# Value projection of the second attention: weights stationary, then transposed, with VectorE writing the rows

## The reference, cut to what matters

```python
def shared_kv(h, w_kv, f_bias, k_gain):
    k, v, fl = jnp.split(h @ w_kv, [B_W, 2 * B_W], axis=-1)
    k = rms_norm(k.reshape(B, T, B_HEADS, HEAD_DIM), k_gain)
    v = v.reshape(B, T, B_HEADS, HEAD_DIM)
    log_f = jax.nn.log_sigmoid(fl + f_bias)
    c = jnp.cumsum(log_f, axis=1).transpose(0, 2, 1)
    return k, v, c

def fox_attention(h, w_q, q_gain, w_out, k, v, c):
    q = rms_norm((h @ w_q).reshape(B, T, B_HEADS, HEAD_DIM), q_gain)
    ...   # scores + decay from c, causal mask, softmax, p @ v, then @ w_out
```

## Time and profile before

| | |
|---|---|
| time, 3 runs | 2240.07 us median (2239.18 to 2240.89) |
| span of the profiled execution | 2240.1 us |
| PE busy | 2018.0 us (90%) |
| DVE busy | 1583.8 us (71%) |
| ACT busy | 1114.1 us (50%) |
| mean granted TensorE clock | 0.984 |

### The profile page before, as it was taken

How to read it: one execution, slowest core, us unless ns; L and a number is a source line. 1 busy time by engine, 2 the same in 40 slices (tenths; PEclk the granted TensorE clock), 3 DMA queues, 4 the chain that set the end, 5 groups by cost and what they waited for, 6 DMA issues and landing times.

```text
span 2240.1 us, 28570 instructions
## 1 busy us (share of the span) xinstructions
PE 2018.0 (90%) x9930; PEld 1294.1 (58%) x9930; DVE 1583.8 (71%) x3680; ACT 1114.1 (50%) x2715; POOL 629.8 (28%) x621
## 2 busy tenths in 40 slices
PE   8899999999999989888779989988999998788876
PEld 7789999789999975433234434433444443233322
DVE  7857778768788888666676586567567666776655
ACT  5456436466534465454445475444356544444543
POOL 0000011100011044344333343344234344444442
PEclk9899999999999999999999999999999999999999
DMA  6226698726598579999999999999999999999997
GB/s 236 77 92 204 221 343 284 256 84 212 195 357 303 188 282 419 421 421 421 421 421 421 421 416 417 414 421 418 398 418 404 421 421 421 421 421 405 422 420 292
DMA packets 130773, 764.58 MB, mean 341 GB/s; under 512 B 14416, under 2 KB 16208, under 8 KB 59088
## 3 DMA queue, kind: packets, MB, share of 16 engines
q0 software_dynamic: 87552, 587.24, 64.3%
q1 hardware_dynamic: 42368, 174.15, 21.4%
q10 hardware_dynamic: 720, 1.51, 0.2%
HBM read 761.80 MB, written 1.05 MB: 341 GB/s over the span
## 4 chain that ended last, share of the span: by engine, by line
PE 50%; DMA 30%; DVE 11%; ACT 5%; issue 3%; POOL 1%; DVEq 0%; POOLq 0%; ACTq 0%
DMA arena<-experts,arena 27%; PE bank L1092 14%; PE bank L599 9%; PE bank L601 8%; PE bank L600 8%; PE bank L1130 6%; DVE arena L2686 3%; DMA wring<-w_stream 1%; DVE wlo L1993 1%; DMA arena<-ada_w 1%; ACT arena L1711 1%; PE bank L783 1%; ACT arena L1495 1%; POOL arena L570 1%; ACT arena L1710 1%
## 5 line engine op out<-in xcount | busy, mean ns | idle before, releaser
L1092 PE MATMUL bank<-arena 128*128 128x512 f32 x2048 | 975.8, 615 | 161.7 <-ACT arena L1711 159.9
L2686 DVE CUSTOM_DVE_ANT_0 arena<-arena 128x1024 f32<-128x1024 f32 x512 | 626.3, 1225 | 449.7 <-DMA arena<-experts,arena 448.9
L570 POOL DMA_INDIRECT arena<-experts,arena x512 | 565.7, 1105 | 841.3 <-PE bank L1092 782.1
L1092 PEld LDWEIGHTS bank<-arena 128*128 128x128 f32 x2048 | 372.7, 193 | 716.3 <-issue 360.8
L1706 ACT ACTIVATE arena<-arena 128x1 f32<-128x1 f32 x512 | 103.4, 202 | 583.3 <-DVE arena L2686 581.4
L1382 ACT CAST whi<-wring 128x1024 fp32r<-128x1024 f32 x229 | 239.1, 1050 | 226.3 <-PE bank L601 220.9
L1993 DVE TENSOR_TENSOR wlo<-wring,whi 128x1024 fp32r<-128x1024 f32 x229 | 278.9, 1223 | 68.7 <-ACT whi L1382 67.9
L1711 ACT ACTIVATE arena<-tab,arena 128x128 f32<-128x128 f32 x512 | 205.5, 401 | 16.7
L550 POOL DMA_DIRECT2D arena<-ada_w x64 | 34.4, 537 | 575.0 <-DVE adaM L2040 561.8
L599 PE MATMUL bank<-hTh,whi 128*128 128x256 f32 (+1 forms) x584 | 169.9, 291 | 1.9 <-DVE wlo L1993 1.3
L601 PE MATMUL bank<-hTh,wlo 128*128 128x256 f32 (+1 forms) x584 | 165.2, 283 | 0.0
(11 more groups left out here) (407 smaller groups left out, 2903.2 us busy)
## 6 DMA issues: line engine op xcount, KB each, us to landing
wring<-w_stream SPq DMA_DIRECT2D x233, 512.0 KB, 4.3
wring<-w_stream SPq DMA_DIRECT2D x46, 1024.0 KB, 9.1
arena<-ada_w POOLq DMA_DIRECT2D x64, 512.0 KB, 5.5
alibi<-ada_w POOLq DMA_DIRECT2D x32, 512.0 KB, 5.6
arena<-experts,arena POOLq DMA_INDIRECT x512
xT<-xT_in SPq DMA_DIRECT2D x2, 544.0 KB, 4.3
alibi<-alibi_in ACTq DMA_DIRECT2D x1, 1024.0 KB, 6.0
tab<-tab_in SPq DMA_DIRECT2D x1, 847.0 KB, 10.5
```

Source lines behind the costliest of these rows:

```text
L570: pool.indirect_dma_start(g_ring[:, r], None, experts[n // (2 * PEER_HEADS)], bass.IndirectOffsetOnAxis(idx[:, s // SLOTS % 2, s % SLOTS:s ...
L1092: last = mm(banks[2 * t + b][:, :], diag[:, r], g_ring[:, r, D + b * TILE_N:D + (b + 1) * TILE_N], start=s % SLOTS == 0, stop=s % SLOTS == ...
L2686: v.tensor_tensor_reduce(g_ring[:, r, 0:D], g_ring[:, r, 0:D], hrow[:, t], 1.0, 0.0, ALU.mult, ALU.add, act8[:, r:r + 1]).then_inc(dot_don ...
```

## The change

The weights become the stationary operand. `value_chunk(n)` makes 128 value columns for all 272 tokens with 24 matmuls, so there are eight chunks instead of 12 groups. ScalarE copies each chunk, unscaled, to a new double-buffered tile `vTB` (`value_copied`). TensorE turns it by three transposes into a bank (`value_turn`), and VectorE multiplies by `kv_ri` and writes `vB` (`value_scaled`, two instructions). The six scaled ScalarE copies go. The order around this is rewritten on the three engines. The release of the ring's chunks for tiles 27 and 28 goes from two halves to each chunk. In the changed program the lines after the new code have other numbers: 600 to 602 are the three matmuls, 986 `head_spread`, 1037 the transposes, 2017 `split_lo`, 2064 `ada_part`, 2383 `head_scale`, 2401 to 2405 `decay_rows`, 2432 and 2433 `value_scaled`.

```diff
-CHUNK_FREE.update({g: (2, 2, 4, 4) for g in (G_BV, G_BV + 1)})
...
+        vTB = m(2, T)
...
-        BV_BANKS = ((0, 1, 2), (4, 7, 6))
+        VALUE_BANK = (0, 1, 2, 3, 6, 7, 6, 7)
+        TURN_BANK = (4, 4, 4, 4, 4, 5, 4, 6)
...
                     if layer and n == 0:
-                        pe.wait_ge(v_ready, 7)
+                        pe.wait_ge(v_ready, 10)
...
             beside_values = attention(1)
-            for n in range(12):
-                x, half, r = n // 6, n // 3 % 2, n % 3
...
-                rows(G_BV + x, c0, TILE_N // 2, banks[BV_BANKS[x][r]][0:nq, c0:c0 + TILE_N // 2],
-                     parts(kvh, kvl, q0, q0 + nq), ((0, 0, 2), (1, 0, 1))[half][r])
-                if n == 0:
-                    head_sums(14)
-                if n < 2:
-                    head_spread(6 + n)
-                elif n < 6:
-                    head_spread(2 * n + 4)
-                    head_spread(2 * n + 5)
-                elif n == 6:
...
-                    next(beside_values)
-                elif n == 8 or n == 10:
-                    next(beside_values)
+            def value_chunk(n):
...
+                chunk(G_BV + n // CPT, n % CPT, banks[VALUE_BANK[n]][:, 0:T], kv_all)
+            def value_turn(n):
...
+                else:
+                    pe.wait_ge(v_ready, 3 + (CPT + 1 if n == CPT + 2 else n))
+                pe.wait_ge(z_copied, 17 + n)
+                for r, (q0, nq) in enumerate(ROWS):
+                    last = nc.tensor.transpose(banks[TURN_BANK[n]][0:nq, r * P:(r + 1) * P], vTB[:, n % 2, q0:q0 + nq], ident)
+                last.then_inc(kv_done, 1)
+            value_chunk(0)
+            head_sums(14)
+            head_spread(6)
+            value_chunk(1)
+            value_turn(0)
+            head_spread(7)
+            head_spread(8)
+            head_spread(9)
+            value_chunk(2)
+            value_turn(1)
+            for n in range(10, 13):
+                head_spread(n)
+            value_chunk(3)
+            value_turn(2)
+            for n in range(13, 16):
+                head_spread(n)
+            value_chunk(4)
+            value_turn(3)
...
+            next(beside_values)
+            value_chunk(5)
+            value_turn(4)
+            next(beside_values)
+            value_chunk(6)
+            value_turn(5)
+            value_chunk(7)
+            value_turn(6)
+            value_turn(7)
+            next(beside_values)
... ScalarE
+            def value_copied(n):
+                act.wait_ge(lin_done, CPT * G_BV + n + 1)
+                if n >= 2:
+                    act.wait_ge(kv_done, n)
+                nc.scalar.copy(vTB[:, n % 2], banks[VALUE_BANK[n]][:, 0:T]).then_inc(z_copied, 1)
             beside_values = attention(1)
-            split_hi(G_BV + 1, 0, 2)
-            split_hi(G_BV + 1, 1, 2)
-            values_copied(0, 0)
...
+            for c in range(CPT):
+                value_copied(c)
+                split_hi(G_BV + 1, c)
+            value_copied(4)
             next(beside_values)
+            value_copied(5)
+            split_hi(G_BOUT, 0)
             next(beside_values)
+            value_copied(6)
+            split_hi(G_BOUT, 1)
+            value_copied(7)
+            split_hi(G_BOUT, 2)
             next(beside_values)
+            split_hi(G_BOUT, 3)
... VectorE
+            def value_scaled(n):
+                cols, bank = slice(n * P, (n + 1) * P), banks[TURN_BANK[n]]
+                dve.wait_ge(kv_done, n + 2)
+                v.tensor_scalar(vB[0:N_META, 0, cols], bank[0:N_META, 0:P], kv_ri[0:N_META, 0:1], None, ALU.mult)
+                v.tensor_tensor(vB[:, 1:3, cols], bank[:, P:3 * P].rearrange("p (r c) -> p r c", r=2),
+                                kv_ri[:, 1:3].unsqueeze(2).to_broadcast([P, 2, P]), ALU.mult).then_inc(v_ready, 1)
             split_lo(G_BV + 1, 0)
+            value_scaled(0)
+            head_scale(10)
+            decay_sums()
             split_lo(G_BV + 1, 1)
-            for x in range(2, 8):
-                head_scale(8 + x)
-                if x == 3:
-                    decay_sums()
-                elif x == 5:
-                    decay_rows()
-            for _ in range(4):
-                ada_part()
+            ada_part()
+            value_scaled(1)
+            head_scale(11)
+            head_scale(12)
+            decay_rows()
             split_lo(G_BV + 1, 2)
+            ada_part()
+            value_scaled(2)
+            head_scale(13)
+            head_scale(14)
+            head_scale(15)
             split_lo(G_BV + 1, 3)
+            ada_part()
+            value_scaled(3)
+            ada_part()
             beside_values = attention(1)
...
```

More of the change, by code:

```diff
@@ L405, in build @@
         relu_done, h1_done = sem("relu_done"), sem("h1_done")
-        wf_landed, wf_hi, wf_split, f_done = sem("wf_landed"), sem("wf_hi"), sem("wf_split"), sem("f_done")
+        wf_landed, wf_hi, wf_split, kv_done = sem("wf_landed"), sem("wf_hi"), sem("wf_split"), sem("kv_done")
         z_copied, head_rt, head_ri, head_bc, head_done = (
@@ L750, in values_b @@
                     if n == 0:
-                        pe.wait_ge(v_ready, 9)
+                        pe.wait_ge(v_ready, 11)
                     pe.wait_ge(ot_split, outs(1, n) - 5)
@@ L999, in _ @@
                 last = mm3(banks[6][0:16, 0:T], (wfh[:, kc], wfl[:, kc]), kv_all(kc), kc == 0, kc == KC - 1)
-            last.then_inc(f_done, 1)
+            last.then_inc(kv_done, 1)
             pe.wait_ge(hn_split, 24)
@@ L1013, in _ @@
             beside_values = attention(1)
-            for n in range(12):
-                x, half, r = n // 6, n // 3 % 2, n % 3
[L1016 to L1020, removed]
-                    elif n == 6:
-                        pe.wait_ge(head_ri, 1)
-                    elif n == 7:
-                        pe.wait_ge(head_done, 16)
-                rows(G_BV + x, c0, TILE_N // 2, banks[BV_BANKS[x][r]][0:nq, c0:c0 + TILE_N // 2],
-                     parts(kvh, kvl, q0, q0 + nq), ((0, 0, 2), (1, 0, 1))[half][r])
-                if n == 0:
-                    head_sums(14)
-                if n < 2:
-                    head_spread(6 + n)
-                elif n < 6:
-                    head_spread(2 * n + 4)
-                    head_spread(2 * n + 5)
[L1034 to L1039, removed]
-                    next(beside_values)
-                elif n == 8 or n == 10:
-                    next(beside_values)
@@ new lines, in value_chunk @@
+            def value_chunk(n):
+                if n < CPT:
+                    pe.wait_ge(z_copied, 13 + n)
+                elif n < CPT + 2:
+                    pe.wait_ge(head_done, 11 + n)
+                else:
+                    pe.wait_ge(z_copied, 15 + n)
+                chunk(G_BV + n // CPT, n % CPT, banks[VALUE_BANK[n]][:, 0:T], kv_all)
+            def value_turn(n):
+                if n == 0:
+                    pe.wait_ge(head_ri, 1)
+                elif n == CPT + 1:
+                    pe.wait_ge(head_ri, 2)
+                elif n == 2 * CPT - 1:
+                    pe.wait_ge(z_copied, 23)
+                else:
+                    pe.wait_ge(v_ready, 3 + (CPT + 1 if n == CPT + 2 else n))
+                pe.wait_ge(z_copied, 17 + n)
+                for r, (q0, nq) in enumerate(ROWS):
+                    last = nc.tensor.transpose(banks[TURN_BANK[n]][0:nq, r * P:(r + 1) * P], vTB[:, n % 2, q0:q0 + nq], ident)
+                last.then_inc(kv_done, 1)
@@ L1043, in _ @@
+            pe.wait_ge(head_done, 10)
+            pe.wait_ge(c_ready, 1)
+            pe.wait_ge(ident_ready, 2)
+            next(beside_values)
[8 more added lines that the diff above has]
+            next(beside_values)
             for _ in range(7):
@@ L2365, in token_inverses @@
                 link(v.reciprocal(fz[0:16, 2], fz[0:16, 1]))
-                dve.wait_ge(f_done, 1)
+                dve.wait_ge(kv_done, 1)
                 v.tensor_tensor(fz[0:16, 3], banks[6][0:16, 0:T], fz[0:16, 2], ALU.mult).then_inc(fz_done, 1)
@@ L2403, in _ @@
             head_scale(9)
+            def value_scaled(n):
[4 more added lines that the diff above has]
+                                kv_ri[:, 1:3].unsqueeze(2).to_broadcast([P, 2, P]), ALU.mult).then_inc(v_ready, 1)
             split_lo(G_BV + 1, 0)
+            value_scaled(0)
+            head_scale(10)
+            decay_sums()
             split_lo(G_BV + 1, 1)
-            for x in range(2, 8):
-                head_scale(8 + x)
-                if x == 3:
-                    decay_sums()
-                elif x == 5:
-                    decay_rows()
-            for _ in range(4):
-                ada_part()
-            split_lo(G_BV + 1, 2)
+            ada_part()
[3 more added lines that the diff above has]
+            decay_rows()
+            split_lo(G_BV + 1, 2)
+            ada_part()
[3 more added lines that the diff above has]
+            head_scale(15)
```

(10 more changed lines are left out.)

17 lines of the change are left out of this document (removed).

## The result

The changed kernel takes 2244.79 us, the median of 20 runs (2242.47 to 2249.75); the kernel before takes 2240.91 us beside it (20 runs, 2236.61 to 2249.49). The ratio is 1.0020, with a 95% interval of 1.0014 to 1.0026: slower by 4.5 us (3.1 to 5.8; the two medians as they stand differ by 3.9), on the very bound between "within 0.2%" and "slower by over 0.2%". The forecast was 2245.7 us, +5.6.

What follows compares the result with a forecast made beforehand. TensorE was taken to bound the value stage, then ScalarE's start of unit 3's exponentials. The order's +2.6 us plus 1.7 and 1.3 for two clock falls gave +5.6 on 2240.1: 2245.7 us, range 2242.2 to 2248.2.

Steps and rivals of the forecast that it cites:

- the two large pauses: TensorE idles 2.4 us ahead of spread 8, for the queries' reciprocal, and 4.6 us ahead of spread 15, for scale 13.
- both falls of the clock: TensorE's clock falls to half at the 2.4 us and 4.6 us pauses, costing 1.3 and 1.7 us.
- the mark: Start of unit 3's exponentials on ScalarE, 462.02 us before; what moves it moves the kernel's end.
- TensorE's saving: In the value stage TensorE's own work falls by 35.9 - 25.7 - 3.2 = 7.0 us.
- Value writes: VectorE's value_scaled, two instructions, costs 0.6 us each time; eight are 4.8 us.
- The rival of dearer writes: VectorE's value writes cost 1.0 us each instead of 0.6: 1.6 us more, 2247.3; chance 0.06.
- Steps 1 to 3: TensorE waits in the value stage: 2.4 us (spread 8), 0.8 (spread 12), 0.6 (turn 2), 0.3 (spreads 13, 14), 4.6 (spread 15).
- Steps 4 and 5: From spread 15 (441.3) to unit 2's scores (458.7) and unit 3's exponentials (464.6, was 462.02): +2.6 us without the clock.
- the 0.2 for the output cast: Ahead of unit 3's exponentials, 0.2 us for an output that ScalarE now waits for inside unit 3.
- Step 6, the clock: TensorE at half clock costs 1.7 us for the 4.6 us pause and 1.3 for the 2.4 us one.
- The rival of one fall: The 2.4 us pause ahead of spread 8 leaves TensorE's clock at full: +4.3 us, 2244.4; chance 0.31.
- The rival of the faster kernel: TensorE stays the bound, 8.7 us of pauses vanish, unit 3's exponentials start at 455.9, 6 us early: 2234; chance 0.05.

Runs made afterwards that it cites:

- e2: The changed kernel with VectorE's value_scaled(2) and head_scale(13) to (15) moved ahead of decay_rows, a split and ada_part: 2241.50 us, 1.0008 of before.
- e6: The changed kernel with 4 idle matmuls ahead of head_spread(8) and 9 ahead of head_spread(15), filling both pauses: 2242.04 us, 1.0004 of before.
- e5: e4 with ScalarE's last weight split moved from ahead of unit 3's exponentials to behind unit 8: 2234.16 us, 0.9971 of before.
- e4: The changed kernel reordered: chunk or turn behind each spread pair, chunk 4 in bank 5, VectorE's value writes and scales before splits and ada_part: 2233.98 us, 0.9971 of before.
- e7: The changed kernel with idle matmuls filling only the pause ahead of head_spread(15): 2243.16 us (one run).
- e1: The changed kernel with 8 idle matmuls ahead of head_spread(8) and 17 ahead of head_spread(15), longer than the pauses: 2246.07 us, 1.0025 of before.
- e3: The changed kernel with value_chunk(2) ahead of head_spread(8) and (9), and VectorE's split_lo and value_scaled(0) ahead of head_scale(8) and (9): 2241.84 us, 1.0003 of before.

## Why the prediction was right

The direction, the two large pauses and, in the one profile of the changed kernel, both falls of the clock came as forecast, and the sum was 5.6 against +5.3 at the mark (+5.4 by distance) and +4.5 (3.1 to 5.8) in time. That the end moves by what the mark moves holds only roughly: by distance and by time it is +0.8 and +1.8 in e2, +1.7 and +0.9 in e6, -5.8 and -6.5 in e5, with some 2 us to either side for each of these times. Step by step:

**TensorE's saving.** A turn is 422.02 to 422.44 = 0.42 us for three transposes (0.40 forecast), so the 24 cost 3.4 us. The Trainium skill (TensorE: Matmul & The Clock Gate, Part 4: PE-mode transpose) has about 275 ns for one of 128x128 in bf16 in a kernel; an estimate by that figure is 6.6 us for the 24. The trace agrees for the length of one (0.27 us here, in fp32) but not for the sum, since transposes that follow one another overlap. A chunk is 418.91 to 422.02 = 3.11 us; the 0.1 that I had added for another kind of matmul on both sides was not there. The saving of 7.0 us was thus a little low (35.9 - 8 x 3.11 - 3.4 = 7.6), and e4 shows that most of it arrives at the mark once nothing gives it away.

**Value writes.** 0.59 us each, 0.6 forecast; the broadcast factor costs nothing that can be seen. The rival of dearer writes falls.

**Steps 1 to 3.** The waits were 2.26, 0.67, 0.45 and 4.44 us; the forecast said 2.4, 0.8, 0.6 and 4.6, and named what each would wait for. A fifth, of 0.3 ahead of spreads 13 and 14, did not come. In e6, whose clock stays up, spread 15 starts 440.86 - 418.69 = 22.17 us behind the start of chunk 1; the forecast, without clock, put it 441.3 - 419.04 = 22.26 behind.

**Steps 4 and 5.** From spread 15 to unit 2's scores the forecast had 17.4 us, and e6 has 457.82 - 440.86 = 16.96: four chunks with 0.1 too much each. From the scores to unit 3's exponentials it had 5.9. In the changed kernel it is 467.33 - 461.74 = 5.59; the 0.2 for the output cast was not on this path. So without the clock the sum was +2.6 forecast and +1.7 measured (e6).

**Step 6, the clock.** Here the error is on the other side. After against e6, the first low stretch delays spread 15 by (442.60 - 418.91) - 22.17 = 1.52 us (forecast 1.3), and the rest up to unit 2's scores by (461.74 - 442.60) - 16.96 = 2.18 (forecast 1.7). The second low stretch was 6.83 us long, and 2.0 us of it lay in the wait. Together 3.7 in place of 3.0. Two terms were off by 0.9 and 0.7 us, and they cancelled.

**The rival of one fall** (+4.3) is not dead. The profile of after shows two, e7 none behind a pause of the same length. If the first fall comes in some executions and not in others, the median lies between the one-fall and the two-fall case; the measured +4.5 would fit that. The mean granted clock that the runs list for whole executions does not settle it: it is 0.9787 over the 20 of after and 0.9812 over the 20 of e1 and e6 together, a difference near the 0.0023 of two stretches (half of 10.24 us in 2243), but e2, whose profile has one stretch of 3.41 us, lies as low (0.9785). It stays open, since only one execution of each kernel is profiled.

**The rival of the faster kernel** (TensorE bound throughout, unit 3's exponentials 6 us early) was rightly excluded for the order as it was written, and its mechanism is real. With that order changed, e4 and e5 reach 5.5 and 5.8 us by distance (e4 without its low stretch) and -6.5 in time.

## What to carry to other kernels

Saving work on the engine that is the bound brings nothing if that work was the cover for another engine's instruction. Lay out both engines' instructions in order, with their prices, and look for the one that is next needed and stands behind a long block that nobody waits for; moving it ahead was worth nearly all of the loss here, and more than all of it when both places were mended. Price a pause of TensorE together with what its clock does behind it: here the half clock cost 3.7 us beside some 7.3 (an estimate) for the waits, against a saving of 5.5 at the mark.

## What the runs showed of the hardware

**A pause's length did not tell whether the clock falls.** It was at 0.50 behind pauses of 2.26 us (after, e2), 3.87 (e3) and 1.68 (e4), from inside one of 4.44 on (after), and behind a wait of only 0.34 (e3, from 430.91), and stayed at 1.00 behind one of 2.30 (e7). The forecast of the first fall leaned on the pause of 2.00 us in the earlier trace rows; no length of a pause that decides shows in these runs.

**An fp32 matmul with 256 columns runs as two instructions** in `fill`: 0.44 us for one (17 of them are x34 in e1's row), where one of the stage's matmuls on the split parts with 256 columns takes 0.13 (24 in 3.04 us). A filling has to be priced from its own rows.
